# Third block's chunk inverse: the last two levels on their own rows and columns, operands of 88 partitions instead of 128

## What is computed

```python
def gated_delta_rule(q, k, v, beta, g):
    ...
    decay = jnp.exp(jnp.where(tril, gc[..., :, None] - gc[..., None, :], NEG_INF))
    kb = k * beta[..., None]
    vb = v * beta[..., None]
    lmat = jnp.where(strict, jnp.einsum('bhncd,bhnsd->bhncs', kb, k) * decay, 0.0)
    eye = jnp.eye(CHUNK, dtype=jnp.float32)
    rhs = jnp.concatenate([vb, kb * jnp.exp(gc)[..., None]], axis=-1)
    sol = lax.linalg.triangular_solve(lmat + eye, rhs, left_side=True, lower=True, unit_diagonal=True)
    value, k_cumdecay = sol[..., :dv], sol[..., dv:]
    attn_intra = jnp.einsum('bhncd,bhnsd->bhncs', q, k) * decay
    ...
    state, o = lax.scan(step, state0, ...)
```

## Time and profile before

| | |
|---|---|
| Median of three runs | 2982.79 us |
| The profiled execution: its own time | 2994.56 us |
| its span | 2993.3 us |
| TensorE matmul busy | 2846.2 us, 95% |
| VectorE busy | 1591.6 us, 53% |
| mean granted TensorE clock | 0.957 |
| the chunk stage | from 2100.9 to 2313.1 us of the span, 212 us (7%) |

### The profile page before, as it was taken

How to read it: one execution, slowest core, us unless ns; L and a number is a source line. 1 busy time by engine, 2 the same in 40 slices (tenths; PEclk the granted TensorE clock), 3 DMA queues, 4 the chain that set the end, 5 groups by cost and what they waited for, 6 DMA issues and landing times. The chain is left out here.

```text
span 2993.3 us, 42636 instructions
## 1 busy us (share of the span) xinstructions
PE 2846.2 (95%) x16674; PEld 2393.0 (80%) x16674; DVE 1591.6 (53%) x2426; ACT 1061.7 (35%) x1809; POOL 608.7 (20%) x487
## 2 busy tenths in 40 slices
PE   8989999999999999989999999999898999999998
PEld 6769877778888766757788888976787899999986
DVE  5854557366553464834433338865344335576643
ACT  4352333432222323252422225444343232422223
POOL 2530101121100121440100003344454000111101
PEclk9977899999999999989999999998899899999999
DMA  4200231122222311202222222210000022222221
GB/s 156 91 1 7 71 106 63 43 92 92 99 92 99 110 64 68 88 9 84 92 92 95 95 92 79 72 36 1 6 2 2 32 90 78 86 92 92 89 95 64
DMA packets 60308, 210.62 MB, mean 70 GB/s; under 512 B 7927, under 2 KB 8567, under 8 KB 59991
## 3 DMA queue, kind: packets, MB, share of 16 engines
q1 hardware_dynamic: 58934, 207.39, 19.7%
q10 hardware_dynamic: 1184, 0.59, 0.1%
HBM read 205.84 MB, written 2.10 MB: 69 GB/s over the span
## 5 line engine op out<-in xcount | busy, mean ns | idle before, releaser
L272 PE MATMUL ps<-normed_hi,slab_hi 128*128 128x264 f32 (+2 forms) x2568 | 869.7, 339 | 27.4 <-DVE normed_lo L576 13.5
L274 PE MATMUL ps<-normed_hi,slab_lo 128*128 128x264 f32 (+2 forms) x2568 | 854.0, 333 | 0.0
L273 PE MATMUL ps<-normed_lo,slab_hi 128*128 128x264 f32 (+2 forms) x2568 | 853.1, 332 | 0.0
L153 ACT ACTIVATE slab_hi<-ring 128x1024 fp32r<-128x1024 f32 x376 | 397.5, 1058 | 1012.3 <-PE ps L274 1000.1
L157 DVE TENSOR_TENSOR slab_lo<-ring,slab_hi 128x1024 fp32r<-128x1024 f32 x360 | 479.5, 1334 | 385.6 <-ACT slab_hi L153 385.1
L272 PEld LDWEIGHTS ps<-normed_hi,slab_hi 128*128 128x128 f32 x2568 | 488.3, 190 | 95.2 <-issue 34.3
L273 PEld LDWEIGHTS ps<-normed_lo,slab_hi 128*128 128x128 f32 x2568 | 488.5, 190 | 52.3 <-issue 4.3
L274 PEld LDWEIGHTS ps<-normed_hi,slab_lo 128*128 128x128 f32 x2568 | 486.7, 190 | 49.1
L272 PE MATMUL ps<-hidden_hi,slab_hi 128*128 128x512 f32 x560 | 220.8, 394 | 5.6 <-DVE hidden_lo L223 5.6
L274 PE MATMUL ps<-hidden_hi,slab_lo 128*128 128x512 f32 x560 | 223.2, 399 | 0.0
L273 PE MATMUL ps<-hidden_lo,slab_hi 128*128 128x512 f32 x560 | 220.9, 395 | 0.0
(11 more groups left out here) (571 smaller groups left out, 4048.4 us busy)
## 6 DMA issues: line engine op xcount, KB each, us to landing
ring<-in_stream SPq DMA_DIRECT2D x376, 512.0 KB, 3.2
h<-in_x SPq DMA_DIRECT2D x8, 256.0 KB, 5.9
mix_y<-in_sgu_b SPq DMA_DIRECT2D x1, 1024.0 KB
out_features<-ffn_hidden SPq DMA_DIRECT2D x2, 512.0 KB, 3.2
xn<-in_c_recip_count SPq DMA_DIRECT2D x1, 512.0 KB, 3.4
rwkv_a<-in_mem SPq DMA_DIRECT2D x1, 512.0 KB, 4.0
rwkv_b<-in_mem SPq DMA_DIRECT2D x1, 512.0 KB, 5.1
sgu_ln<-in_sgu_ln SPq DMA_DIRECT2D x1, 512.0 KB
```

Source lines behind the costliest of these rows:

```text
L153: self.nc.scalar.activation(self.hi[:, n % PARTS, :], self.ring[:, n % SLOTS, :], ACT.Copy).then_inc(self.hi_ready, 1)
L272: nc.tensor.matmul(to, lhsT[0], rhs[0], start=start, stop=False)
L273: nc.tensor.matmul(to, lhsT[0], rhs[1], start=False, stop=False)
L274: return nc.tensor.matmul(to, lhsT[1], rhs[0], start=False, stop=stop)
```

## The change

All six buffers have 88 partitions, no clearing and no semaphore `padded`; the matmuls read 88 partitions. The new helper `sides(l)` gives, for l = 4, rows and columns 0 to 31 (`up`) and 32 to 63 (`down`), for l = 5 0 to 63 and 64 to 87, and for the levels before the whole 88. The turn, both products, both copies and the addition of a level take only these. GpSimd's mask instructions stay at 88x352.

```diff
@@ -3366,11 +3366,10 @@
     with ExitStack() as local:
         masks_in = K.buf(local, "gdn_masks", [C3, LEVELS_G + 5, C3])
 
-        wide_prod, wide_amask, wide_inv, wide_invT = wides = [K.buf(local, n, [P, 2, QUAD, C3]) for n in ("gdn_prod", "gdn_A_level", "gdn_inv", "gdn_invT")]
-        wide_bv, wide_bk = wide_rhs = [K.buf(local, n, [P, 2, QUAD, HD]) for n in ("gdn_beta_v", "gdn_beta_k")]
-        prod, amask, inv, invT, bv, bk = (t[0:C3] for t in wides + wide_rhs)
+        prod, amask, inv, invT = (K.buf(local, n, [C3, 2, QUAD, C3]) for n in ("gdn_prod", "gdn_A_level", "gdn_inv", "gdn_invT"))
+        bv, bk = (K.buf(local, n, [C3, 2, QUAD, HD]) for n in ("gdn_beta_v", "gdn_beta_k"))
         amat, beta_mask = (K.buf(local, n, [C3, 2, QUAD, C3]) for n in ("gdn_A", "gdn_beta_mask"))
-        arrived, chain, pool_chain, padded = (K.sem(n) for n in ("gdn_masks_arrived", "gdn_chain", "gdn_pool_chain", "gdn_padded"))
+        arrived, chain, pool_chain = (K.sem(n) for n in ("gdn_masks_arrived", "gdn_chain", "gdn_pool_chain"))
         (sums_filled, keys_filled, queries_filled, split, exped, weighted, first, attn_out, firstT_filled, firstT, masked, turned, inv_out,
          z_filled, z_out, d_filled, d_added, x_filled, x_out, rhs_ready) = ([K.sem(f"gdn_{n}_{q}") for q in range(2)] for n in (
             "sums_filled", "keys_filled", "queries_filled", "split", "exped", "weighted", "first", "attn_out", "firstT_filled", "firstT", "masked", "turned",
@@ -3385,8 +3384,20 @@
         def own(t, c, q):
             return t[0:C3, c, q:GDN_HEADS:2, :]
 
-        def bank(q, b):
-            return K.ps[0:C3, 4 * q + b, 0:QUAD * C3].rearrange("p (h i) -> p h i", i=C3)
+        def bank(q, b, rows=C3, columns=C3):
+            return K.ps[0:rows, 4 * q + b, 0:QUAD * C3].rearrange("p (h i) -> p h i", i=C3)[:, :, 0:columns]
+
+        def sides(l):
+
+
+
+            if l < LV - 2:
+                return slice(0, C3), slice(0, C3)
+            n = 32 << l - (LV - 2)
+            return slice(0, n), slice(n, min(2 * n, C3))
+
+        def width(x):
+            return x.stop - x.start
 
         def head(base, h, c):
             rows = slice((h % 2) * HD, (h % 2 + 1) * HD)
@@ -3445,6 +3456,7 @@
                     last.then_inc(firstT_filled[q], 1)
 
                 def product(c, q, l, n):
+                    up, down = sides(l)
                     if l == 0:
                         pe.wait_ge(firstT[q], c + 1)
                     else:
@@ -3452,33 +3464,33 @@
                         pe.wait_ge(d_added[q], n)
                         pe.wait_ge(attn_out[q], c + 1)
                         for i in range(QUAD):
-                            last = nc.tensor.transpose(bank(q, 2)[:, i, :], invT[:, q, i, :], K.ident[0:C3, 0:C3])
+                            last = nc.tensor.transpose(bank(q, 2)[up, i, up], invT[up, q, i, up], K.ident[up, up])
                         last.then_inc(turned[q], 1)
                     pe.wait_ge(masked[q], n + 1)
                     for i in range(QUAD):
-                        last = nc.tensor.matmul(bank(q, 0)[:, i, :], wide_amask[:, q, i, :], wide_invT[:, q, i, :], start=True, stop=True)
+                        last = nc.tensor.matmul(bank(q, 0)[up, i, 0:width(down)], amask[:, q, i, up], invT[:, q, i, down], start=True, stop=True)
                     last.then_inc(z_filled[q], 1)
 
                 def add(c, q, l, n):
                     pe.wait_ge(z_out[q], n + 1)
                     if l:
                         pe.wait_ge(inv_out[q], c * (LV - 1) + l)
+                    up, down = sides(l)
                     for i in range(QUAD):
-                        last = nc.tensor.matmul(bank(q, 1)[:, i, :], wide_inv[:, q, i, :], wide_prod[:, q, i, :], start=True, stop=True)
+                        last = nc.tensor.matmul(bank(q, 1)[up, i, 0:width(down)], inv[up, q, i, up], prod[up, q, i, 0:width(down)], start=True, stop=True)
                     last.then_inc(d_filled[q], 1)
 
                 def result(c, q):
                     pe.wait_ge(d_added[q], LV * (c + 1))
                     pe.wait_ge(rhs_ready[q], c + 1)
                     for i in range(QUAD):
-                        last = nc.tensor.matmul(K.ps[0:HD, 4 * q + 2, i * C3:(i + 1) * C3], wide_bk[:, q, i, :], wide_invT[:, q, i, :], start=True, stop=True)
+                        last = nc.tensor.matmul(K.ps[0:HD, 4 * q + 2, i * C3:(i + 1) * C3], bk[:, q, i, :], invT[:, q, i, :], start=True, stop=True)
                     last.then_inc(x_filled[q], 1)
                     for i in range(QUAD):
-                        last = nc.tensor.matmul(K.ps[0:C3, 4 * q + 3, i * HD:(i + 1) * HD], wide_invT[:, q, i, :], wide_bv[:, q, i, :], start=True, stop=True)
+                        last = nc.tensor.matmul(K.ps[0:C3, 4 * q + 3, i * HD:(i + 1) * HD], invT[:, q, i, :], bv[:, q, i, :], start=True, stop=True)
                     last.then_inc(x_filled[q], 1)
 
                 warm(K, 0, 4)
-                pe.wait_ge(padded, len(wides + wide_rhs))
                 run(pairs=pairs, turn=turn, product=product, add=add, result=result)
 
             @block.vector
@@ -3517,11 +3529,10 @@
                 def add(c, q, l, n):
                     dve.wait_ge(d_filled[q], n + 1)
                     dve.wait_ge(firstT[q], c + 1)
-                    nc.vector.tensor_tensor(invT[:, q], bank(q, 1), invT[:, q], ALU.add).then_inc(d_added[q], 1)
-
-                for t in wides + wide_rhs:
-                    nc.vector.memset(t[HD:P], 0.0).then_inc(padded, 1)
-                dve.wait_ge(padded, len(wides + wide_rhs))
+                    up, down = sides(l)
+                    at = invT[up, q, :, down]
+                    nc.vector.tensor_tensor(at, bank(q, 1)[up, :, 0:width(down)], at, ALU.add).then_inc(d_added[q], 1)
+
                 dve.wait_ge(arrived, 16)
                 run(pairs=pairs, triangle=triangle, turn=turn, product=product, add=add)
 
@@ -3541,11 +3552,12 @@
                     nc.scalar.activation(invT[:, q], bank(q, 3), ACT.Copy).then_inc(firstT[q], 1)
 
                 def product(c, q, l, n):
+                    up, down = sides(l)
                     if l:
                         act.wait_ge(turned[q], c * (LV - 1) + l)
-                        nc.scalar.activation(inv[:, q], bank(q, 2), ACT.Copy).then_inc(inv_out[q], 1)
+                        nc.scalar.activation(inv[up, q, :, up], bank(q, 2)[up, :, up], ACT.Copy).then_inc(inv_out[q], 1)
                     act.wait_ge(z_filled[q], n + 1)
-                    nc.scalar.activation(prod[:, q], bank(q, 0), ACT.Copy).then_inc(z_out[q], 1)
+                    nc.scalar.activation(prod[up, q, :, 0:width(down)], bank(q, 0)[up, :, 0:width(down)], ACT.Copy).then_inc(z_out[q], 1)
 
                 def add(c, q, l, n):
                     pass
@@ -3598,7 +3610,6 @@
 
                         nc.gpsimd.tensor_tensor(keys, keys, over(3, c, q, HD), ALU.mult).then_inc(rhs_ready[q], 1)
 
-                pool.wait_ge(padded, len(wides + wide_rhs))
                 pool.wait_ge(arrived, 16)
                 run(pairs=pairs, triangle=triangle, product=product, add=add, result=result)
 
```

## The result

| | before | after |
|---|---|---|
| median of 4 runs each | 2989.7 us (2976.0 to 2998.22) | 3097.38 us (3088.63 to 3098.89) |
| ratio, 95% interval | 1 | 1.032 (1.030 to 1.035) |
| profiled execution: own time, span | 2994.56, 2993.3 us | 3097.91, 3096.6 us |
| mean granted TensorE clock | 0.957 | 0.914 |
| chunk stage | 212.5 us | 306.6 us |

The chunk stage is counted here, in every kernel alike, from the issue of its masks' transfer to the first instruction of the scan. The page of after answers to the earlier trace rows: as many records, 107 us more of busy time, and in the clock's row, of 40 slices of 77 us each, four stand at 5, half speed, and the one behind them at 7.

The account below looks back on a forecast made before the run. TensorE, busy 95% of the span, was taken to bound the kernel. The stage's +68.5 and the scan's +4 gave +72.5, which on the median 2982.79 made 3055 us, range 3000 to 3080.

Parts of the forecast that it names:

- part 4: One unit (one chunk, one group) at half clock: 21.9 us; 44.4 a chunk against 31.7, +63.5 us over five.
- Clearing: Start of the chunk stage: without clearing and its wait, TensorE starts earlier, -0.7 us.
- The clock: Chunk stage: 88-row matmuls would leave TensorE's clock at 0.50 until the scan; by themselves fewer rows save nothing.
- The small levels: Levels 4 and 5 of each unit at half clock: 2.5 us against 5.9 whole, less 1.4 for ten size changes.
- A change of size: Gap on TensorE where an operand's rows or columns change: 0.14 us each, ten new ones per unit, 1.4 us.
- Rival C: Chunk stage: 32-row records cost 0.147 us and size changes 0.23; up to +45 us, half giving 3078; no separate chance.
- Filling and tail: Stage before the first result and after group 0's last: +3.5 and -0.7 at the start, +2.2 in the tail.
- The scan: Start of the scan stage: it begins at half clock until 128-row matmuls lift it, +1 to +8, taken as +4 us.
- A (clock as today): Chunk stage: 88 rows count like 128 for the clock, -6 us, 2977 us; chance 0.10.
- B: Chunk stage: dense 88-row work lifts the clock, small levels and pairs drop it; half the loss, 3019 us; chance 0.12.

Follow-up runs that it names:

- rows88: The kernel before with 88 partitions instead of 128 and no clearing, all levels whole: 3110.59 us, ratio 1.036.
- rows96: The kernel before with 96 partitions instead of 128, levels whole: 3111.24 us, executed once.
- rows112: The kernel before with 112 partitions instead of 128, levels whole: 3005.77 us, ratio 1.001.
- l4only88: The changed kernel with only level 4 cut and level 5 whole: 3099.60 us, executed once; stage 308.2 us.
- l5only88: The changed kernel with only level 5 cut and level 4 whole: 3113.11 us, executed once; stage 320.3 us.
- small_padded: The kernel before, with 128 rows and clearing kept, levels 4 and 5 cut to their rows and columns: ratio 1.000.
- small128: The kernel before, with 128 rows and whole turns kept, levels 4 and 5 cut in columns alone: ratio 0.999.
- burst88: The changed kernel plus four 128-row, 512-column matmuls on constants ahead of group 0's level 3 in the first chunk: 3091.97 us, executed once.

## Why the prediction was off

It said 3055 us, with 3000 to 3080 as the range; 3097.38 lies 17 us outside. Direction and mechanism were right, the size was not. The step that failed is part 4's sum for a chunk at half clock, 44.4 us, where 49.2 were measured: level 5's records, the waits, the changes of size and the result were all priced too low. In the order of its parts:

1. **Clearing: right.** TensorE's first 8-row product stands 3.5 us behind the stage's start (2112.59, first row below) and stood 4.15 behind it before (2105.05 in the earlier trace rows, the stage from 2100.9): -0.65, forecast -0.7.

2. **The clock: right.** Half clock from 2117.6 into the scan, records of full products 1.17 us apart. rows88 and rows96 show that it hangs on the partitions. The rule from the earlier trace rows, 8 and 64 rows don't lift and 128 do, with 88 nearer to 64, held; what decides lies between 96 and 112. That 88 would go with 64 was taken from nearness alone, and no row showed it, so that much was luck. The reading of the 8-row stretch was also not exact. The clock did not stay at 0.50 there: it stood at 1.00 while 8-row products already ran (nearly all of the 23 records below), and fell with TensorE busy throughout. The trace of before thus showed not only that few rows don't lift the clock, but that dense work of few rows can lose it:

```profile
2075.80:2079.20 3.40, 3.40 (x23) 2.87 (x23) 0.71 (x3) 0.50 (x3) 1.72 (x1) 1.00 0.00 0
```

The Trainium skill, "TensorE: Matmul & The Clock Gate", Part 1 (The HAM clock gate), has the clock follow TensorE's recent busyness. Where busy is what the profile shows as busy, this case's runs disagree. The same dense stretch at the same place, first in rows96, then in rows112 with what followed it:

```profile
2137.80:2141.20 3.40, 3.40 (x24) 3.40 (x25) 0.79 (x2) 1.05 (x3) 2.00 (x3) 0.50 0.00 0
2141.20:2144.60 3.40, 3.40 (x25) 3.40 (x24) 0.52 (x1) 1.07 (x3) 2.16 (x3) 0.50 0.00 0
```

```profile
2139.20:2142.60 3.40, 3.40 (x24) 3.40 (x25) 0.88 (x2) 1.05 (x3) 1.99 (x3) 0.50 0.00 0
2142.60:2146.00 3.40, 3.40 (x44) 3.32 (x43) 1.04 (x2) 1.75 (x5) 2.28 (x4) 1.00 0.00 0
```

In both TensorE was busy throughout with the same 24 records, line by line, one version with 96 rows in its products and the other with 112; behind it the kernel with 112 rows went on at 1.00, with 44 records in the next 3.4 us, and the one with 96 rows at 0.50.

3. **The small levels: here a term was mis-sized.** TensorE in order of time, after, through both of them and the result behind:

```profile
2112.59 0.85 PE L3438 MATMUL ps<-head_rates,square_constants 8*88 8x88 f32 x8
...
2140.40 0.39 PE L3467 MATMUL ps<-square_constants,gdn_invT 32*32 32x32 f32 x4
2140.72 0.64 PE L3471 MATMUL ps<-gdn_invT,gdn_A_level 88*32 88x32 f32 x8
2141.28 2.04 PE L3480 MATMUL ps<-gdn_prod,gdn_inv 88*88 88x88 f32 x16
2143.37 0.81 PE L3467 MATMUL ps<-square_constants,gdn_invT 88*88 88x88 f32 x4
2143.98 1.38 PE L3471 MATMUL ps<-gdn_invT,gdn_A_level 88*88 88x88 f32 x8
2145.29 0.63 PE L3467 MATMUL ps<-square_constants,gdn_invT 64*64 64x64 f32 x4
2145.85 1.05 PE L3471 MATMUL ps<-gdn_invT,gdn_A_level 88*64 88x24 f32 x8
2146.83 2.45 PE L3480 MATMUL ps<-gdn_prod,gdn_inv 88*88 88x88 f32 x16
2149.22 0.81 PE L3467 MATMUL ps<-square_constants,gdn_invT 88*88 88x88 f32 x4
...
2151.13 1.44 PE L3487 MATMUL ps<-gdn_invT,gdn_beta_k 88*64 88x88 f32 x8
2152.50 1.44 PE L3490 MATMUL ps<-gdn_beta_v,gdn_invT 88*88 88x64 f32 x8
2153.73 1.42 PE L3480 MATMUL ps<-gdn_prod,gdn_inv 88*88 88x88 f32 x8
```

(A row of L3480 x16 is a full product and a small one behind each other.) Level 5's first product starts at 2145.85 and the next group at 2146.83: 0.98 us for eight records, of which the changes of size are 0.12; the records lie 0.107 us apart, not 0.06. With 64 columns in the array and 24 streamed, the wider of the two sets the price, the same 0.107 as 64x64 with 64 streamed. The forecast took 0.077 from a weight load of 88 columns with 8 streamed and scaled it down. But that row is of 18 turns (L3308), which leave one record each, and not of products. A product with few streamed columns stood in the same trace, at full clock:

```profile
2076.14 1.95 PE L3313 MATMUL ps<-last_sum,square_constants 8*128 8x6 f32 x16
```

The next line starts at 2077.95, so its records lie 0.113 us apart with 6 columns streamed, about as far as the eight of L3633 in the earlier trace rows do with 128 (0.94 us to the next line, 0.117 each). A row that lay near was also the result's in the earlier trace rows: 88 columns in the array, 64 streamed. The distance from L3477 to the next line there, 0.68 for eight, is a wide record's price in spite of its narrower stream (0.63 for a full product, and a change of size in it). Level 4's records lie 0.053 us apart, forecast 0.055.

A change of size is worth more than 0.14. The first record behind it waits that long, and the second of a full product often has 0.1 more. From l4only88: level 4's 20 records at 0.053 instead of 0.147 save 1.9 us a unit, measured are 1.05, so five changes take 0.83, 0.17 each. From l5only88: 20 records at 0.107 save 0.8, measured is 0.03, which leaves 0.15 each. In the mean it is 0.16. Rival C had 0.23 for the change, and 0.147 for the small records; both were too high.

4. **The unit.** The gap between 49.2 and 44.4 us for a chunk comes apart like this:

| | us a chunk |
|---|---|
| level 5's 32 product records at 0.107, not 0.06 | 1.5 |
| 20 new changes of size at 0.16, not 0.14 | 0.4 |
| the result's L3490 at 1.17 us for eight, not 0.86 | 0.6 |
| waits 0.82 + 0.76 + 0.32 = 1.9, not 0.6 | 1.3 |
| old changes of size and hand-overs 2.4, not 1.4 (51.3 - 320 x 0.147 - 1.9, rows88) | 1.0 |
| sum; measured 4.8 | 4.8 |

So 1.5 of the 4.8 us are level 5's records, and 2.9 lie in parts that the change doesn't touch, which had been priced from full-clock rows or rounded down. Five chunks make 24 us. The forecast of the saving, level by level, was 2.3 us a chunk for level 4 (measured 2.1) and 1.7 for level 5 (measured 0.05).

5. **Filling and tail: near.** The first result stands 43.4 us behind the stage's start for 39.9, +3.5 (forecast +2.8); the tail is 2413.31 - 2398.42 = 14.9 us for 12.3, +2.6 (forecast +2.2).

6. **The scan: +2.0 for +4.** The start of the scan before, then after; the last row of after answers to the earlier trace rows:

```profile
2313.20 1.95 PE L281 MATMUL ps<-square_constants 128*128 128x512 f32 x4 [0.72 <-PEq L326]
...
2317.55 1.16 PE L3638 MATMUL ps<-gdn_new_values,gdn_k_tok 128*128 128x128 f32 x8 [0.18 <-DVE gdn_new_values L3662]
```

```profile
2415.47 3.75 PE L281 MATMUL ps<-square_constants 128*128 128x512 f32 x4 [0.72 <-PEq L326]
2419.01 1.92 PE L3644 MATMUL ps<-gdn_state,gdn_kcdT 128*88 128x128 f32 x8
...
2421.77 1.16 PE L3649 MATMUL ps<-gdn_new_values,gdn_k_tok 128*128 128x128 f32 x8
...
2425.42 1.11 PE L3644 MATMUL ps<-gdn_state,gdn_kcdT 128*88 128x128 f32 x8
```

Four records on constants took 3.75 us for 1.95, and the first product 1.92 for 1.11; but a wait of 0.44 us for VectorE before that product is hidden now. From the first constants to the second product of the scan it is 6.30 us for 4.35, so +2.0. Behind these 128-row matmuls the clock is back, at 2421.4.

**The sum.** The stage grew by 94.1 us, forecast 68.5: 24 of the 25.6 are part 4's table, 1.1 filling and tail. The rest of the program, the scan's start among it, is 9.2 us longer, forecast 4. Its code is the same in every kernel here, and in their traces it takes 2776.4 to 2792.5 us, so beyond the scan's 2.0 us nothing of it can be put down to the change. The miss against the medians, 42 us, is larger than the stage's for two reasons: 5 us from this rest, and 11.8 us which the forecast had taken off for a profiled execution slower than its runs, which the runs of after didn't repeat (theirs lies 0.5 above its median).

**The rivals.** A (clock as today) is refuted by rows88. What it would have been is seen with 128 rows: at full clock the small levels take 0.35 us off a chunk, 2.3 us over its 6.5 chunks, within its 1 to 6 though nearer to the low end. B fell with rows88, small_padded and small128. C's upper prices were both too high: 0.23 for a change of size, where 0.16 was measured and the forecast had 0.14, and 0.147 for a 32-row record, where 0.053 was measured. What was more than forecast lay elsewhere.

## What to carry to other kernels

Rows of zeros are not always waste: before a padded operand is cut to its real partitions, look at what stretches of such products do to the granted clock, for the loss (a full product 1.17 us instead of 0.63 through a whole stage, 94 us longer in after) dwarfs the clearing (0.7 us). Price each record of a float32 product by the wider of its two sides, columns in the array or columns streamed, as the shapes measured here went (a turn need not: L3308's records with 88 and 8 columns lie 0.073 us apart), and each change of size between neighbours with it; a cut of one side alone, or one that brings five changes for 20 records, may save nothing. When a stage starts with a wait that lets the clock fall, matmuls on constants in that wait can be worth more than thinner work.

## What the runs showed that was not expected

- The dependence on partitions looks graded, from one trace each: 96 rows 317 us at half clock in one piece, 104 rows 58 us in seven pieces, 112 rows 51 in four, 128 rows 34 in four.
- The work of the 88-row kernel kept a lifted clock for 15.4 us before it fell (burst88).
- Between 88 and 128 partitions, with 88 columns, the rows make no difference to a full product's price: 1.17 us for its eight records at half clock (rows88, before) and 0.63 us at full clock (burst88, before).
- The kernel before spends 34 us of its chunk stage at half clock, and filler makes the stage 8.3 us shorter.
